# Two mixture-of-experts layers: the last pair's up weights gathered in four pieces, stores that skip unused rows, and a new order of copies and weighings at each layer's end

## The reference

```
def hier_moe(x, w_group, b_group, w_expert, b_expert, w_gate, w_up, w_down):
    t = x.reshape(B * S, D)
    g_val, g_idx = top_k(softmax(t @ w_group + b_group), 1)          # 1 of 4 groups
    e_val, e_idx = top_k(softmax(logits of that group's 4 experts), 2)   # 2 of 4 experts
    e_val = e_val / sum(e_val)
    combine = g_val * e_val at expert g_idx * 4 + e_idx, else 0
    hid = silu(t @ w_gate[e]) * (t @ w_up[e]) * combine              # 256 wide
    out = sum over e of hid @ w_down[e]
```

## Time and profile before

| | |
|---|---|
| median of 3 runs | 2359.68 us (2359.5 to 2360.51) |
| the profiled execution's own time | 2356.8 us |
| its span | 2355.0 us |
| PE busy | 2264.7 us (96%) |
| DVE, ACT, POOL busy | 1294.8, 1247.5, 212.1 us |
| mean granted TensorE clock | 0.995 |
| DMA | 339.43 MB, mean 144 GB/s |

### The profile page before, as it was taken

The page is one execution under the profiler, slowest core; times in us unless marked ns, Lnnn a source line. Parts: engine busy times, 40 slices in busy tenths (PEclk is TensorE's granted clock), DMA queues, the critical chain, the costliest instruction groups (busy, mean ns, idle before and its releaser), DMA issues.

```text
span 2355.0 us, 30152 instructions
## 1 busy us (share of the span) xinstructions
PE 2264.7 (96%) x11756; PEld 1083.7 (46%) x11756; DVE 1294.8 (55%) x2618; ACT 1247.5 (53%) x2227; POOL 212.1 (9%) x290
## 2 busy tenths in 40 slices
PE   7999999999999999999999999999999999999997
PEld 3434554444444454444444446554334444554333
DVE  5565856456555456776654684653326744644323
ACT  7544666667557575666665764522216664421213
POOL 0000000000000430000000000102221000001231
PEclk9999999999999999999999999999999999999999
DMA  5230011222222211222223221459974231438996
GB/s 201 90 110 1 1 72 72 108 108 74 99 105 110 78 66 46 91 98 107 85 99 121 84 96 55 198 183 378 415 303 148 74 142 40 163 108 352 421 416 249
DMA packets 68334, 339.43 MB, mean 144 GB/s; under 512 B 11730, under 2 KB 12040, under 8 KB 53836
## 3 DMA queue, kind: packets, MB, share of 16 engines
q1 hardware_dynamic: 51120, 266.62, 29.4%
q0 software_dynamic: 17072, 70.88, 8.1%
HBM read 367.67 MB, written 23.10 MB: 166 GB/s over the span
## 4 chain that ended last, share of the span: by engine, by line
PE 85%; DVE 6%; ACT 4%; DMA 3%; issue 2%; POOL 0%; DVEq 0%; SPq 0%; POOLq 0%; ACTq 0%
PE PB L406 12%; PE PB L401 12%; PE PB L407 12%; PE PB L3367 8%; PE PB L3393 4%; PE PB L1732 3%; PE PB L1736 3%; PE PB L1733 3%; PE PB L452 2%; PE PB L454 2%; PE PB L453 2%; PE PB L3319 1%; DMA T<-moe_x,small 1%; DVE WS L321 1%; PE PB L3975 1%
## 5 line engine op out<-in xcount | busy, mean ns | idle before, releaser
L406 PE MATMUL PB<-AS,WS 128*128 128x512 f16 x1352 | 512.5, 379 | 1.3 <-DVE WS L321 1.3
L407 PE MATMUL PB<-AS,WS 128*128 128x512 f16 x1352 | 512.4, 379 | 0.0
L401 PE MATMUL PB<-AS,WS 128*128 128x512 f16 x1352 | 484.7, 379 | 2.5 <-DVE AS L1201 2.5
L321 DVE SCALAR_TENSOR_TENSOR WS<-raw,sc,WS 128x1024 f16<-128x1024 f32 (+3 forms) x288 | 328.2, 1188 | 88.8 <-ACT WS L308 88.8
L308 ACT ACTIVATE WS<-raw,sc 128x1024 f16<-128x1024 f32 (+3 forms) x288 | 288.5, 1057 | 71.3 <-DVE sc L288 71.1
L262 ACT ACTIVATE junk<-raw 128x1024 f16<-128x1024 f32 (+3 forms) x288 | 280.0, 972 | 7.0
L3367 PE MATMUL PB<-T 128*64 128x512 f32 x736 | 217.7, 603 | 20.3 <-issue 10.3
L406 PEld LDWEIGHTS PB<-AS,WS 128*128 128x128 f16 x1352 | 132.3, 98 | 163.8 <-issue 5.5
L401 PEld LDWEIGHTS PB<-AS,WS 128*128 128x128 f16 x1352 | 132.3, 98 | 163.0 <-DVE AS L1201 4.1
L407 PEld LDWEIGHTS PB<-AS,WS 128*128 128x128 f16 x1352 | 132.3, 98 | 159.0 <-issue 3.0
L3527 ACT ACTIVATE T<-PB 128x256 f32<-128x256 f32 (+1 forms) x32 | 12.1, 378 | 283.4 <-PE PB L3367 273.2
(11 more groups left out here) (654 smaller groups left out, 3629.6 us busy)
## 6 DMA issues: line engine op xcount, KB each, us to landing
T<-in_moe_up SPq DMA_DIRECT2D x26, 2048.0 KB, 12.8
raw<-in_w_up SPq DMA_DIRECT2D x22, 2048.0 KB, 7.7
T<-in_moe_down SPq DMA_DIRECT2D x26, 1024.0 KB, 14.5
raw<-in_w_down SPq DMA_DIRECT2D x16, 1408.0 KB, 6.0
raw<-in_w_in_even SPq DMA_DIRECT2D x8, 2048.0 KB, 7.8
raw<-in_w_in_odd SPq DMA_DIRECT2D x8, 2048.0 KB, 7.6
moe_y<-X SPq DMA_DIRECT2D x28, 512.0 KB, 11.4
WS<-in_moe_up SPq DMA_DIRECT2D x6, 2048.0 KB, 16.0
```

Source lines behind the costliest of these rows:

```text
L321: e.scalar_tensor_tensor(lo[q], raw[q], s, hi[q], MUL, SUB).then_inc(*k.s("dve_split").up("lo", i, q))
L401: return e.matmul(bank, wh[:, q, c, :], act.lo[c], start=False, stop=c == kt - 1)
L406: e.matmul(bank, wh[:, q, c, :], act.hi[c], start=c == 0, stop=False)
L407: e.matmul(bank, wl[:, q, c, :], act.hi[c], start=False, stop=False)
```

## The change

1. `up(15)`'s weights are gathered as four DMAs of 1 MB in place of two of 2 MB: the first half of every partition's 16 KB for both units, then the second half for both. DVE computes their indices (`half_i`) with two small instructions. PE waits for the first half's two before the first matmul and for the second half's two before the 17th.
2. The blocks 6, 9, 11, 12 and 13 (`scattered`) are stored by POOL with an indirect DMA, one index for each row; an unused row's index is out of bounds. DVE computes them with two small instructions at two places. SP no longer stores these. Block n's store stands in POOL's program in iteration n+2 behind the gather of x.
3. The rows of `moe_y` of these five blocks are zeroed ahead too (ten more stores of 64 rows).
4. ACT's order at the end of a layer becomes last(0), weigh(0), last(1), weigh(1), then for each quarter mean, square and root, with weigh(2) ahead of quarter 1 and weigh(3) ahead of quarter 2. DVE's becomes part(0), total(0), part(1), total(1), part(2), total(2), part(3).

```diff
-    for u in range(2):
-        o = 128 * ORDER[NB - 1] + 64 * u
-        e.dma_start(k.out_d[layer][o:o + 64, :], m.xT[0][0:64, :]).then_inc(*k.s("out_zero").dma(layer))
+    for n in range(NB):
+        if n == NB - 1 or scattered(n):
+            for u in range(2):
+                o = 128 * ORDER[n] + 64 * u
+                e.dma_start(k.out_d[layer][o:o + 64, :], m.xT[0][0:64, :]).then_inc(*k.s("out_zero").dma(layer))
...
+def scattered(n):
+
+    return not experts(n) and n != LONE and n < NB - 2
+
+
+def stored(k, n):
+
+    return k.s(f"out_used{n % 2}" if scattered(n) else f"out_y{n % 2}")
...
         if n > 0:
-            sp_moe_out(k, e, w, layer, n - 1)
+            if not scattered(n - 1):
+                sp_moe_out(k, e, w, layer, n - 1)
...
     def up(b):
-        for u in range(2):
-            w.wait_ge(*k.s(f"in_up{slot(b, u)}" if experts(b) else f"in_more_up{slot(b, u)}").past(layer, b))
+        if b < NB - 1:
+            for u in range(2):
+                w.wait_ge(*k.s(f"in_up{slot(b, u)}" if experts(b) else f"in_more_up{slot(b, u)}").past(layer, b))
...
         for c in range(KT):
             for u in range(2):
+                if b == NB - 1 and c % 4 == 0:
+                    w.wait_ge(*k.s(f"in_half_up{c // 4}{u}").past(layer))
...
     def down(b):
         w.wait_ge(*p.past("down", b, 0))
         if b >= 2:
-            w.wait_ge(*k.s(f"out_y{b % 2}").past(layer, b - 2))
+            w.wait_ge(*stored(k, b - 2).past(layer, b - 2))
...
-    weigh(0)
-    weigh(1)
-    for half in range(2):
+    def last(half):
         w.wait_ge(*p.past("down", NB - 1, half))
...
-    weigh(2)
-    weigh(3)
+
+    last(0)
+    weigh(0)
+    last(1)
+    weigh(1)
     for q in range(4):
+        if q in (1, 2):
+            weigh(q + 1)
...
+        if b0 >= NB // 2:
+            e.tensor_scalar(m.free[:, b0:b1], PB[7][:, b0:b1], 0.0, 4096.0, ALU.is_equal, MUL).then_inc(*v.up("free", b0))
+            w.wait_ge(*v.now())
+            e.scalar_tensor_tensor(m.y_i[:, b0:b1], m.free[:, b0:b1], 128.0 * b0, m.tok, ADD, ADD).then_inc(
+                *v.up("used", b0))
...
+    o = 2 * ORDER[NB - 1] - NE
+    for half in range(2):
+        e.tensor_scalar(m.half_i[:, 2 * half:2 * half + 2], m.w_f[:, o:o + 2], 2.0, float(half), MUL, ADD).then_inc(
+            *v.up("half_i", half))
...
     part(0)
+    total(0)
     part(1)
+    total(1)
     part(2)
-    total(0)
-    total(1)
+    total(2)
     part(3)
-    total(2)
...
+            if b + 2 == NB - 1:
+                halves = k.ins[f"moe_up{layer}"].rearrange("r (h c) -> (r h) c", h=2)
+                for half in range(2):
+                    w.wait_ge(*v.past("half_i", half))
+                    for u in range(2):
+                        at = bass.IndirectOffsetOnAxis(m.half_i[:, 2 * half + u:2 * half + u + 1], 0)
+                        e.indirect_dma_start(m.gu[slot(b + 2, u)][:, 2048 * half:2048 * half + 2048], None, halves, at,
+                                             bounds_check=2 * 128 * NE - 1, oob_is_err=False).then_inc(
+                            *k.s(f"in_half_up{half}{u}").dma(layer))
+                return
...
     for b in range(NB):
         load_x(b + 2)
+        if b >= 2 and scattered(b - 2):
+            n = b - 2
+            w.wait_ge(*k.s("out_zero").past(layer))
+            w.wait_ge(*v.past("used", 4 * (ORDER[n] // 4)))
+            w.wait_ge(*a.past("down", n))
+            w.wait_ge(*v.past("down", n))
+            at = bass.IndirectOffsetOnAxis(m.y_i[:, ORDER[n]:ORDER[n] + 1], 0)
+            e.indirect_dma_start(k.out_d[layer], at, m.yst[n % 2], None, bounds_check=128 * NB - 1, oob_is_err=False).then_inc(
+                *stored(k, n).dma(layer, n))
```

More of the change, by code:

```diff
@@ L3217, in moe_at @@
         top1, top2, many, den, w1, w2 = (k.small[:, a:a + 4] for a in (132, 136, 140, 144, 148, 152))
-        pos_i, w_i, x_i = (k.small[:, o:o + n].bitcast(U32) for o, n in ((256, 8), (264, NU - NE), (288, NB)))
+        pos_i, w_i, x_i, y_i = (k.small[:, o:o + n].bitcast(U32) for o, n in ((256, 8), (264, NU - NE), (288, NB), (304, NB)))
+        free = k.small[:, 304:304 + NB]
+        half_i = k.small[:, 304:308].bitcast(U32)
         upto, all_ = k.PB[6][:, 0:64], k.PB[6][:, 64:80]
@@ L3273, in sp_moe_out @@
             e.dma_start(k.out_d[layer][o:o + 64, 512 * u:512 * u + 512], m.yst[b % 2][64 * u:64 * u + 64, 0:512]).then_inc(
-                *k.s(f"out_y{b % 2}").dma(layer, b))
+                *stored(k, b).dma(layer, b))
     else:
-        e.dma_start(k.out_d[layer][o:o + 128, :], m.yst[b % 2]).then_inc(*k.s(f"out_y{b % 2}").dma(layer, b))
+        e.dma_start(k.out_d[layer][o:o + 128, :], m.yst[b % 2]).then_inc(*stored(k, b).dma(layer, b))
 def moe_pe(k, e, w, layer):
@@ L3530, in down_lone @@
         w.wait_ge(*p.past("down", LONE))
-        w.wait_ge(*k.s(f"out_y{LONE % 2}").past(layer, LONE - 2))
+        w.wait_ge(*stored(k, LONE - 2).past(layer, LONE - 2))
         e.activation(m.yst[LONE % 2][0:64, 0:512], PB[5][0:64, :], ACT.Copy).then_inc(*a.up("down", LONE))
@@ L3545, in moe_act @@
     e.preload_act_table_set(ROOT)
-    w.wait_ge(*k.s(f"out_y{(NB - 1) % 2}").past(layer, NB - 3))
+    w.wait_ge(*stored(k, NB - 3).past(layer, NB - 3))
     def weigh(q):
@@ L3571, in moe_act @@
     w.wait_ge(*k.s("dve_setup").past("gain"))
-    for j in range(2):
-        w.wait_ge(*k.s(f"out_y{j}").past(layer, NB - 2 - (NB - 2 - j) % 2))
+    for n in (NB - 3, NB - 2):
+        w.wait_ge(*stored(k, n).past(layer, n))
     for i in range(KT):
```

## The result

The changed kernel takes 2348.63 us (median of 5 runs, 2340.51 to 2351.39), the kernel before 2359.68 beside it: ratio 0.9941, 95% interval 0.9927 to 0.9955. 2345.3 had been predicted, 2341.5 to 2351.5. Two further series of the same kernel gave 0.9934 (0.9918 to 0.9951) and 0.9955 (0.994 to 0.9969). The three ratios put the gain at 10.6 to 15.6 us, the medians at 11.1 to 14.1, where 14.4 had been forecast. The 16.3 us between the two spans are therefore more than the gain. The later two profiled executions have spans of 2345.2 and 2347.1 us.

The account below looks back on a forecast made before the run. PE holds 85% of the chain, but full DMA engines deliver expert weights late and PE waits. Layer 0's 2.9 and 3.1 us and layer 1's 8.4 made 14.4 off 2359.7: 2345.3 us, range 2341.5 to 2351.5.

Parts of the forecast that it names:

- rival (a): Shorter gains: stores 11 to 13 save nothing and the clock still falls at layer 0's up(11); 2348.5 us, chance 0.22.
- Layer 0, up(11): Wait shrinks by 1.26 us from 1.97 to 0.7 and the clock stays, 8.77 becoming 7.09: 2.9 us.
- Layer 0, end: last(0) no longer stands behind weigh(1), so PE's 2.57 us wait goes; last total starts 3.1 us sooner.
- Layer 1, bytes: Stores 6 and 9 bring up(15)'s landing 2.5 us forward, 11 to 13 another 1.5; waits of up(11), up(13) dissolve.
- halved guess for stores 11 to 13: Time the DMA engines are spared by skipped rows in layer 1: bounds 0 and 2.99 us, half taken, 1.5.
- Layer 1, pieces: up(15)'s first halves land at 2303.0; 16 matmuls, a 1.4 us wait, end at 2311.6 against 2321.23, clock kept.
- Layer 1, gathers of y: down(14)'s copies wait for store 12; store 14 lands in 5.6 us; first gather of y starts 1.3 us earlier.
- From y to the last total: Layer 1's last total starts 16.85 us after the first gather of y, at 2331.75 against 2340.21: 8.4 us.
- Covered costs: Additional zero stores, small DVE instructions and POOL's store issues fall into idle time; uncovered, zero stores cost up to 6 us.
- (b): Store 12 lands 4 to 6 us behind up(15) and holds layer 1's end; total 2350 us, chance 0.14.
- (c): POOL's scatter lands 18 to 20 us behind up(15), delaying both layers' ends; 2376 us, chance 0.03 alone.
- (d): Unused rows are written all the same, so the byte savings go; 2352 us, chance 0.03.

Follow-up runs that it names:

- scatter alone: The kernel before with only the stores that skip unused rows and their zeroing: ratio 0.9969 to the kernel before.
- order alone: The kernel before with only the new order of ACT's copies and weighings and DVE's parts and totals: ratio 0.9981 to the kernel before.
- all rows: The changed kernel, but its scatters write every row of their block, unused ones too: ratio 0.9961 to the kernel before.
- store 12 ahead: The changed kernel with block 12's scatter issued ahead of up(15)'s pieces on POOL, not behind them: ratio 0.9929 to the kernel before.
- three parts alone: The kernel before with only the four-piece gather, only the scatter or only the new order: ratios 0.9988, 0.9969 and 0.9981 to the kernel before.
- halves alone: The kernel before with only the four-piece gather of the last pair's up weights: ratio 0.9988 to the kernel before.
- block 14 scattered: The changed kernel with block 14 scattered as well, behind down(15)'s gathers and the scatter of 13 on POOL: ratio 0.9952 to the kernel before.
- 12 and 13 by SP: The changed kernel with blocks 12 and 13 stored whole by SP as before: ratio 0.9968 to the kernel before.

## Why the prediction was right, step by step

The median of 2348.63 us lies in the stated range, 3.3 us above the 2345.3 and outside the spread of 2342 to 2347 that was given to the forecast. It is nearly the 2348.5 of rival (a), but (a)'s mechanism is not what the traces show: up(11) of layer 0 kept its clock in all three executions of the changed kernel, and up(15) of layer 1 landed 4.7 and 3.9 us sooner in the two that show it. The sum for the profiled execution was 14.4 us, and that execution gained 16.3. What the sum carried over from the kernel before, 2.9 us between the profiled execution and the median, was 8.1, 0.3 and -0.1 us in the three series of the changed kernel. That term is chance, and so is the closeness of the number; the steps are to be judged by the traces.

- **Layer 0, up(11)**: 2.9 us forecast. The wait shrank by 1.8 us (forecast 1.26) and 1.7 came from the clock, 3.5 in all; up(15) ended 4.3 us sooner. In the two later executions the wait was 0.80 and 0.65 us, where 0.7 was forecast, and up(11) took 7.09 us as well. But the clock's share was partly luck in the execution that it was measured from: in three other kernels with a wait of 1.97, 2.00 or 2.73 us at that place, up(11) kept 7.09 us, so the 1.7 us are not there to be won in every execution of the kernel before. Layer 0 as a whole gained 7.1, 2.7 and 5.0 us in the three executions, with 6.0 forecast; in the later two, 3.3 and 1.8 us of the difference to the first are the stall described in the last section and the clock behind it.
- **Layer 0, end**: 3.1 forecast, 2.8 measured: from up(15)'s end to the last total it is 21.8 us before and with the scatter alone, 19.0 after and with the order alone. The new order does what it was read to do: PE's wait of 2.57 us is gone, and the last total waits 0.35 us for PE.
- **Layer 1, bytes**: 4.0 us forecast to the landing of the whole of up(15), 4.7 and 3.9 measured in two executions. The halved guess for stores 11 to 13 (0 to 2.99 us) held. The wait of up(11) did not dissolve as the prediction had it: it was 1.62 us, and in the later executions 2.25 and 2.41, where the clock fell and the up took 8.8 us. Evenly dealt rows would give 5.5 us. An estimate by the rule of the Trainium skill ("DMA: Bandwidth & Descriptors", "The descriptor swizzle"), which deals a transfer of 128 partitions to the engines in groups of four neighbouring ones, is 3.8 us; no run here shows the dealing. The kernels differ by 3.4 (*scatter alone*) to 6.4 us (*all rows* against the changed one), and equal kernels by 0.8: how rows are dealt to engines stays open here.
- **Layer 1, pieces**: the first 16 matmuls, the wait in the middle (1.4 forecast, 0.73 measured in the first execution) and the kept clock came as written; PE's end at 203.5 to 204.3, where 2311.6 - 2107.5 = 204.1 was forecast.
- **Layer 1, gathers of y**: 1.3 us earlier forecast, 1.2 measured (0.3 to 0.4 in the two later executions). Store 14's landing was put at 5.6 us and took 5.85; that the copies of down(14) would wait for store 12 was right, by 11.08 us. What was wrong is the reason why y starts then: freeing that copy moved nothing by itself.
- **From y to the last total**: the mis-sized term. 16.85 us forecast, 17.8 measured. The third weighing waited until 2319.69 for y4, the fifth gather, which landed 7.5 us behind its issue, not 5.8. From that landing to the last total it is 5.3 us here and in layer 1 of *store 12 ahead* and *all rows*, where y4 took 7.06 and 7.12 us to land and the whole is 17.4 and 17.5. In layer 0 of those two kernels y4 landed 6.1 us behind its issue, and the last total started 16.6 us behind the first gather. So the working of the two engines' order holds, and the error is y4's landing. Why it lands later in layer 1 no run shows. This is why layer 1 gave 7.5 us and not 8.4; in the later executions, with 6.7 and 6.5, the first gather also came 0.8 to 1.0 us later than in the first.
- **Behind the last total**: nothing forecast, since the order there is unchanged; 1.1 us gained. Of the 32 short matmuls, 24 ran ahead of the last total instead of all behind it. It comes from the gathers holding the total and not PE, and it is missing in all three parts alone (14.8 us each).
- **Covered costs and rivals**: the additional zero stores show in no wait; no run has them alone. Rivals (b) and (c), a scatter of block 12 that lands 4 to 20 us behind up(15), did not occur: it landed 0.2 us behind the last piece. (d) is refuted by the 4.59 MB.

## What to carry to other kernels

Where the DMA engines are full and PE is still nearly busy, write the end of a stage as the later of two marks, here the end of PE's last up + 19.0 us and the first gather + 17.4 to 18.4. An edit is worth only what it moves of the later one; here the edits moved both, and together they were worth their sum within the noise. Follow each mark to the end of the program, since one of them can carry work behind it that the other doesn't, 1.1 us here. Where the engines are full, the bytes ahead of a landing count. With a small store ahead of the critical gathers on their queue, not behind them, PE's last up ended 0.9 to 1.7 us later, and the gathers of y started no sooner. In an engine's program, put the copy that PE waits for ahead of operations whose data have still to land.

## What the runs showed of the hardware

- **Short waits and TensorE's clock.** Over the 14 profiled executions, each whole up (one that waits only at its start) after a wait of up to 1.9 us took 7.09 us, at 2.4 GHz throughout (granted clock 1.00). Between 1.97 and 2.96 us nine kept it and eight took 8.68 to 10.07 us, partly at 1.2 GHz (granted clock 0.81, once 0.70). All nine of 3.02 us and more took 8.55 us or longer (0.70 to 0.83). The middle range can thus make executions of one kernel differ by 1.7 us a place, and once by 3.0; that this is a part of the 2 to 12 us between its fastest and slowest run is likely, but not shown.
- **A small scatter behind large gathers.** 11 rows took 14.0 us to land behind 4 MB of its queue's gathers; an empty one by itself 2.1. POOL issued one 0.9 us after the copy it waited for (1765.34 to 1766.21), SP's store started 0.1 us after its own (2300.48 to 2300.55).
- **A stall on two engines at once, not explained.** In three executions (the two later ones of the changed kernel, one with block 14 scattered) the copies of down(13) came late in both layers, though their products were there: on ACT by 1.9 to 3.1 us, on DVE by 1.1 to 1.8. In two more, *halves alone* and *12 and 13 by SP*, ACT's came 1.6 to 2.0 us late and DVE's 0.4 or less. From ACT, DVE and PE of the third series' execution of the changed kernel, layer 0:

```profile
1754.93 0.60 ACT L3539 ACTIVATE X<-PB 128x512 f32<-128x512 f32 x1 [2.81 <-PE PB L3411]
```

```profile
1756.40 0.69 DVE L3736 COPY X<-PB 128x512 f32<-128x512 f32 x1 [3.98 <-PE PB L3395]
```

```profile
1757.48 3.65 PE L3411 MATMUL PB<-T 128*64 128x512 f32 x16 [2.51 <-DVE T L3772]
```

  In the execution with span 2338.7 the same rows show 0.81, 2.22 and 0.76 us. That is 1.1 to 1.8 us for PE in each layer of the three; at three of these six places the clock fell behind it too (5.35 us for the 16 matmuls, granted clock 0.68). The landing of the store of block 11, for which both copies also wait, is missing from the traces that have the stall, so a late landing can't be told from a stall in the engines; no run separates them.
